# Centring and scaling of the layer norms in halves of 512 columns, in a three-layer block on one Trainium2 core

## The chip, the cores and the metric

The kernel runs on one core of one Trainium2 chip. The metric is device time in microseconds (us), lower is better. PE is the matrix engine, PEld its weight load, DVE the vector engine, ACT the scalar engine, POOL and SP the engines that mostly start transfers. Each engine runs its own list of instructions in order and waits for the others on semaphores.

## The reference

Three layers follow each other on 256 tokens of width 1024, all in float32: a gated linear attention with a convolutional MLP, an attention layer (forgetting and stick-breaking heads) with a SwiGLU, and a sliding-window layer with eight experts. What the change touches is the layer norm of the last two layers:

```python
def layer_norm(x, g, b):
    xf = x.astype(F32)
    mu = jnp.mean(xf, axis=-1, keepdims=True)
    xc = xf - mu
    var = jnp.mean(xc * xc, axis=-1, keepdims=True)
    return (xc * lax.rsqrt(var + LN_EPS) * g.astype(F32) + b.astype(F32)).astype(x.dtype)

for i in range(DEPTH_2):                    # 2
    h = fox_sb_mixer(...) or swa_mixer(...)
    x = layer_norm(DEEPNORM_ALPHA * x + h, ln_mix_g[i], ln_mix_b[i])
    h = swiglu(...) or moe_swiglu(...)
    x = layer_norm(DEEPNORM_ALPHA * x + h, ln_ffn_g[i], ln_ffn_b[i])
    x = x + jax.nn.sigmoid(x @ ple_w_gate[i]) * (p[i] @ ple_w_proj[i])
```

## The kernel before

The 256 tokens lie in two tiles of 128 (x[:, t, :]), the 1024 columns along the free dimension. Every product runs with operands split into a high and a low part (w_hi, w_lo of the weights, xt_hi, xt_lo of the activations), three matmuls for one. Weights stream in chunks of 128x2048 through rings of four: SP loads a chunk, ACT rounds it (w_hi, line 641), DVE makes the rest (w_lo, split_chunk, line 1200), PE uses it. A product needs the activations transposed: PE transposes 128x128 pieces into PSUM (L2174, four pieces of one half of 512 columns make one group, t_ready), ACT rounds the group (xt_hi), DVE subtracts (xt_lo, turned, L1212).

There are four layer norms, two tiles each. Three come from follow_norm: after ab_out, after ffn_down and after c_out. For each tile, add_half adds the second half of the product to x (L1288) and takes its statistics (L1290), then normalize(t, i, src) aggregates them (L1296), adds epsilon (L1298), lets ACT take the square root, meanwhile centres the tile and multiplies by the gain (L1301), takes the reciprocal (L1240), multiplies by it and adds the bias (L1303), drains, and raises t_source by 2. The fourth norm follows the experts: add_last and normalize(0), add_last(1), then in ple the two xt_lo groups of tile 0 and normalize(1).

DVE's order around them is written out by hand. After ab_out: norm of tile 0, of tile 1, then the four xt_lo groups (operand(5)) and the rest of p's operand. After ffn_down: tile 0; add_half of tile 1; between the two, first_operand (a chunk's split, xt_lo groups 0 and 1); the rest of tile 1's norm; then in ple the next split, xt_lo groups 2 and 3. After c_out: tile 0, tile 1, the four xt_lo groups (operand(9)), then the router's steps. After the experts, as said; then one split, groups 2 and 3, three splits.

PE's turn_tile(m, src, t) waits for t_source once for each half g, for 4m + 2t + g + 1, and transposes that half. So its two waits per tile are already there; before the change both are met by the one increment of 2. keep_warm issues dummy matmuls (L2179) between the tiles' transposes: 13 after ab_out, 11 after c_out, and 2 behind them. After ab_out PE then begins with the high parts (cols_chunk_high_first, L2134 and L2136) and needs xt_lo only for the last part (L2132). After ffn_down, ple(0) runs matmuls of tile 0 (L2056 to L2058), transposes tile 1, and goes on with the next chunk of tile 0. After c_out the router's matmuls are L2809, L2810 (high) and L2813 (low). After the experts, rows_high_first (L2540, L2541, then L2547 for w_lo) stands in ple(1). The lines of the change are 1300 to 1304.

Of the kernel before, what the change touches and what calls it, by code (L numbers as in the profile page):

```python
# [14 lines left out]
ALU = mybir.AluOpType  # L15
# [12 lines left out]
NB = 512  # L28
# [88 lines left out]
def build(nc, a, out, upto="end"):  # L117
# [27 lines left out]
    with ExitStack() as ctx:  # L145
# [13 lines left out]
        def sb(name, shape, dt=F32):  # L159

            t = at(name, shape, dt, free[0])
            free[0] += nbytes(shape)
            return t
# [11 lines left out]
        def S(name):  # L175

            if name not in sems:
                sems[name] = ctx.enter_context(nc.semaphore(name))
            return sems[name]
# [5 lines left out]
        x = sb("x", [P, NT, D])  # L185
# [15 lines left out]
        stat = sb("stat", [P, 16])  # L201
# [989 lines left out]
        def _(dve):  # L1191
            me = Place()
            dve.sem_inc(S("lo_ready"), RING)
            TT, STT, TS = dve.tensor_tensor, dve.scalar_tensor_tensor, dve.tensor_scalar
# [32 lines left out]
            def row(i):  # L1227
                dve.wait_ge(S(f"gain_landed{i % 2}"), 16 * (i // 2 + i % 2))
                return gain[:, i % 2, :]
# [3 lines left out]
            def inverse_root(tiles=slice(0, NT), meanwhile=None):  # L1233

                dve.drain().then_inc(S("ms_ready"), 1)
                if meanwhile:
                    meanwhile()
                dve.wait_ge(S("root_ready"), next(roots))
                a_, o = (slice(k + tiles.start, k + tiles.stop) for k in (2, 4))
                dve.reciprocal(stat[:, o], stat[:, a_])  # L1240
                dve.drain()
# [50 lines left out]
            def normalize(t, i, src):  # L1292

                g, b_ = row(i), row(i + 1)
                dve.drain()
                dve.bn_aggr(stat[:, 8 + 2 * t:10 + 2 * t], bn[:, t, :, :])  # L1296
                dve.drain()
                TS(stat[:, t:t + 1], stat[:, 9 + 2 * t:10 + 2 * t], LN_EPS, None, ALU.add)  # L1298

                def centred():  # L1300
                    STT(x[:, t, :], src[:, t, :], stat[:, 8 + 2 * t:9 + 2 * t], g, ALU.subtract, ALU.mult)  # L1301
                inverse_root(slice(t, t + 1), centred)
                STT(x[:, t, :], x[:, t, :], stat[:, 4 + t:5 + t], b_, ALU.mult, ALU.add)  # L1303
                dve.drain().then_inc(S("t_source"), 2)

            def follow_norm(name, i, between=None):

                (b0, c0, _, _, p0_), (b1, c1, _, _, p1_) = phase[name]
                round_to(c0 + len(p0_) + 2)
                wait_used(dve, c0 + len(p0_))  # L1310
                for t in range(NT):
                    add_half(0, t, acc[b0 % 2][t])
                dve.drain().then_inc(S(f"acc_free{b0 % 2}"), 1)
                round_to(c1 + len(p1_) + 2)
                for t in range(NT):
                    wait_tile(dve, name, t)
                    add_half(1, t, acc[b1 % 2][t])
                    if t == NT - 1:
                        dve.drain().then_inc(S(f"acc_free{b1 % 2}"), 1)
                        if between:  # L1320
                            between()
                    normalize(t, i, x)
                dve.sem_inc(S("gain_used"), 2)
# [11 lines left out]
            g = gain[:, 0, :]  # L1335
# [69 lines left out]
            for step in range(3):  # L1405
                for g in range(4):
                    src, dst = (step, step + 1) if g < 2 else (3 - step, 2 - step)
# [166 lines left out]
            if "ab_in" in live:  # L1574
# [46 lines left out]
                for h in range(8):  # L1621
                    dve.wait_ge(S("fox_t"), h + 1)
                    dve.tensor_copy(pt[:, h % 2, :], acc[va_b[0] % 2][h % 2][:, 0:SCW]).then_inc(S("fox_pt"), 1)
                    if h in (4, 6):
                        t = h // 2 - 2
# [43 lines left out]
            def ple(i, m, r=0):  # L1669

                blocks = phase[f"ple{i}"]
                if i:
                    turned(m, 0)
                    turned(m, 1)
                    normalize(1, m, y)
                    dve.sem_inc(S("gain_used"), 2)
                    round_to(blocks[0][1] + 3, r)
                    turned(m, 2)
                    turned(m, 3)
                    round_to(blocks[0][1] + 4, r)  # L1680
                else:
                    round_to(blocks[0][1] + 4, r)
                    turned(m, 2)
                    turned(m, 3)
                for q, (bb, cc, n0, n, ps) in enumerate(blocks[2:4]):
                    round_to(cc + len(ps) + 2, r)
                    for t in range(NT):
                        dve.wait_ge(S("sig_ready"), 4 * i + 2 * q + t + 1)
                        TT(sig[:, q, t, :], sig[:, q, t, :], p_out[:, t, n0:n0 + n], ALU.mult)
                        dve.drain()  # L1690
                        k = TT(x[:, t, n0:n0 + n], x[:, t, n0:n0 + n], sig[:, q, t, :], ALU.add)
                        if q and i == 0:
                            dve.drain().then_inc(S("t_source"), 2)
                        elif q and t == 0:
                            dve.drain().then_inc(S("ple_added"), 1)
                    dve.drain().then_inc(S("ple_added"), 1)
# [238 lines left out]
            if "moe" in live:  # L1935
# [92 lines left out]
                dve.drain()  # L2028
                add_last(0)
                normalize(0, 10, y)  # L2030
                add_last(1)
            if "ple1" in live:
# [853 lines left out]
```

## Time and profile before

| | us |
|---|---|
| median of 3 runs | 1815.37 (1813.89 to 1816.74) |
| the profiled execution | 1816.34 |
| its span, first to last instruction | 1814.6 |
| mean granted TensorE clock | 0.995 |
| PE / DVE / ACT busy | 98% / 75% / 61% |

A busy share is an average over the whole span; what matters for this change is who waits for whom in the few microseconds around each norm. The rows further below come from the page (shares and chain), from the chain of waits, from groups of instructions, from timelines (start, duration, engine, line, operation, and in brackets the idle time before it and what ended it) and from busy times by stretch.

### The profile page before, as it was taken

The page shows a single profiled execution, that of the slowest core. Times are in us where ns is not written, and L with a number is a line of the kernel's source. Part 1 is how long each engine was busy: PE and PEld are TensorE (multiplying, and loading weights), DVE is VectorE, ACT ScalarE, POOL GpSimd, SP SyncE. Part 2 cuts the span into 40 slices and gives each one's busy share as a digit, 9 for nine tenths or more (in the row PEclk, how much of TensorE's full clock was granted, in tenths as well). Part 3 has the DMA queues.
Part 4 walks back from the last instruction along what each step waited for, and adds up shares of the span by engine and source line. Part 5 has one row for each costly group of instructions (what it writes and reads, how often), then busy time and mean ns, then how long its engine had stood idle before and what let it go on. Part 6 is the DMA issues. An engine that isn't in the chain of part 4 may idle for free.

```text
span 1814.6 us, 23858 instructions
## 1 busy us (share of the span) xinstructions
PE 1781.8 (98%) x9708; PEld 1500.8 (83%) x9708; DVE 1369.8 (75%) x1199; ACT 1099.2 (61%) x976; POOL 71.5 (4%) x95
## 2 busy tenths in 40 slices
PE   8999999999999999999999999999999999999997
PEld 6979998897899877778788888888888888888886
DVE  4766784466644555689988888888898888888986
ACT  5545563474344344466776776777767777767764
POOL 2200000200000001000000000000000000000100
PEclk8999999999999999999999999999999999999999
DMA  7444556532455564269999999999999999999991
GB/s 260 163 170 151 185 174 221 168 119 98 170 185 184 186 208 140 72 229 386 331 397 380 340 399 357 368 390 349 383 380 345 400 354 368 391 353 377 403 348 71
DMA packets 250471, 496.76 MB, mean 274 GB/s; under 512 B 10630, under 2 KB 15818, under 8 KB 250368
## 3 DMA queue, kind: packets, MB, share of 16 engines
q1 hardware_dynamic: 244992, 477.30, 72.8%
q0 software_dynamic: 4944, 16.50, 2.5%
q8 instruction: 67, 1.10, 0.2%
q10 hardware_dynamic: 432, 1.57, 0.2%
q14 instruction: 36, 0.29, 0.0%
HBM read 489.56 MB, written 5.78 MB: 273 GB/s over the span
## 4 chain that ended last, share of the span: by engine, by line
PE 91%; DVE 5%; issue 1%; DVEq 1%; ACT 1%; DMA 0%; ACTq 0%; SPq 0%
PE psum L2737 17%; PE psum L2739 16%; PE psum L2738 16%; PE psum L2056 5%; PE psum L2151 5%; PE psum L2154 5%; PE psum L2153 5%; PE psum L2058 5%; PE psum L2057 5%; PE psum L2174 3%; DVE w_lo L1769 1%; PE psum L2134 1%; PE psum L2132 1%; PE psum L2136 1%; DVE w_lo L1200 1%
## 5 line engine op out<-in xcount | busy, mean ns | idle before, releaser
L641 ACT ACTIVATE w_hi<-w_raw 128x2048 fp32r<-128x2048 f32 (+1 forms) x357 | 641.0, 1835 | 99.7 <-PE psum L2058 60.4
L1769 DVE TENSOR_TENSOR w_lo<-w_raw,w_hi 128x2048 fp32r<-128x2048 f32 (+1 forms) x236 | 507.0, 2188 | 72.2 <-ACT w_hi L641 72.0
L1200 DVE TENSOR_TENSOR w_lo<-w_raw,w_hi 128x2048 fp32r<-128x2048 f32 (+2 forms) x121 | 266.0, 2230 | 122.3 <-ACT w_hi L641 120.0
L2737 PE MATMUL psum<-w_hi,xg_hi 128*128 128x512 f32 x892 | 356.4, 400 | 1.1 <-DVE w_lo L1769 1.1
L2739 PE MATMUL psum<-w_hi,xg_lo 128*128 128x512 f32 x892 | 352.4, 395 | 0.0
L2738 PE MATMUL psum<-w_lo,xg_hi 128*128 128x512 f32 x892 | 352.2, 395 | 0.0
L1769 DVE TENSOR_TENSOR w_lo<-raw_more,w_hi 128x2048 fp32r<-128x2048 f32 (+1 forms) x116 | 250.2, 2196 | 35.9 <-ACT w_hi L641 35.3
L641 ACT ACTIVATE w_hi<-raw_more 128x2048 fp32r<-128x2048 f32 (+1 forms) x118 | 210.5, 1823 | 16.9 <-PE psum L2739 12.6
L2151 PE MATMUL psum<-xt_hi,w_hi 128*128 128x256 f32 (+2 forms) x768 | 217.2, 283 | 0.0
L2154 PE MATMUL psum<-xt_hi,w_lo 128*128 128x256 f32 (+2 forms) x768 | 216.4, 282 | 0.0
L2153 PE MATMUL psum<-xt_lo,w_hi 128*128 128x256 f32 (+2 forms) x768 | 216.4, 282 | 0.0
L2739 PEld LDWEIGHTS psum<-w_hi,xg_lo 128*128 128x128 f32 x892 | 167.9, 188 | 39.6
L2737 PEld LDWEIGHTS psum<-w_hi,xg_hi 128*128 128x128 f32 x892 | 168.0, 188 | 39.3 <-DVE w_lo L1769 2.0
L2738 PEld LDWEIGHTS psum<-w_lo,xg_hi 128*128 128x128 f32 x892 | 168.1, 188 | 37.5
L2737 PE MATMUL psum<-w_hi,mh_hi 128*128 128x512 f32 x448 | 178.3, 398 | 0.6 <-DVE w_lo L1769 0.5
L2739 PE MATMUL psum<-w_hi,mh_lo 128*128 128x512 f32 x448 | 177.0, 395 | 0.0
L2738 PE MATMUL psum<-w_lo,mh_hi 128*128 128x512 f32 x448 | 176.8, 395 | 0.0
L2151 PEld LDWEIGHTS psum<-xt_hi,w_hi 128*128 128x128 f32 (+2 forms) x768 | 143.4, 187 | 1.3 <-issue 0.8
L2153 PEld LDWEIGHTS psum<-xt_lo,w_hi 128*128 128x128 f32 (+2 forms) x768 | 143.4, 187 | 0.5
L2154 PEld LDWEIGHTS psum<-xt_hi,w_lo 128*128 128x128 f32 (+2 forms) x768 | 143.3, 187 | 0.3
L641 ACT ACTIVATE mg<-psum 128x512 f32<-128x512 f32 x56 | 33.5, 598 | 167.8 <-PE psum L2739 167.8
L2737 PEld LDWEIGHTS psum<-w_hi,mh_hi 128*128 128x128 f32 x448 | 84.4, 188 | 20.2 <-issue 1.2
(438 smaller groups left out, 2285.0 us busy)
## 6 DMA issues: line engine op xcount, KB each, us to landing
w_raw<-in_moe_w_gate_up SPq DMA_DIRECT2D x150, 1024.0 KB, 8.7
raw_more<-in_moe_w_gate_up SPq DMA_DIRECT2D x74, 1024.0 KB, 8.6
w_raw<-in_moe_w_down SPq DMA_DIRECT2D x64, 1024.0 KB, 7.6
raw_more<-in_moe_w_down SPq DMA_DIRECT2D x32, 1024.0 KB, 7.4
w_raw<-in_w_up SPq DMA_DIRECT2D x22, 1024.0 KB, 5.6
w_raw<-in_ffn_w_gate_up SPq DMA_DIRECT2D x22, 1024.0 KB, 5.7
w_raw<-in_w_in SPq DMA_DIRECT2D x12, 1024.0 KB, 5.7
w_raw<-in_ab_w_in SPq DMA_DIRECT2D x12, 1024.0 KB, 5.3
```

The costliest lines, as they stand in the source:

```text
L641: return act.activation(o, i, func, **kw)
L1200: TT(w_lo[:, k % RING, 0:n], raw(slot, n), w_hi[:, k % RING, 0:n].bitcast(F32), ALU.subtract)\
L1769: TT(w_lo[:, at, 0:n], raw(slot, n), w_hi[:, at, 0:n].bitcast(F32), ALU.subtract).then_inc(S("lo_ready"), 1)
L2056: mm(o, hi(k, t), wh, start=(k == ps[0][0]), stop=False)
L2057: mm(o, hi(k, t), wl, start=False, stop=False)
L2058: m = mm(o, lo(k, t), wh, start=False, stop=(k == kmax))
L2151: mm(o, w_hi[:, slot, cols], xt_hi[:, k, :], start=(k == 0 and c_ % 2 == 0), stop=False, skip_group_check=True)
L2153: mm(o, w_hi[:, slot, cols], xt_lo[:, k, :], start=False, stop=False, skip_group_check=True)
L2154: m = mm(o, w_lo[:, slot, cols], xt_hi[:, k, :], start=False, stop=(k == KD - 1), skip_group_check=True)
L2737: mm(o, hi[:, q, :], wh, start=(q == first), stop=False)
L2738: mm(o, hi[:, q, :], wl, start=False, stop=False)
L2739: m = mm(o, lo[:, q, :], wh, start=False, stop=(q == last))
```

## The change

Centring and scaling of a tile are done in two halves of 512 columns (NB). The first half is centred while ACT takes the root, then scaled, drained and announced by raising t_source by 1; then the second half is centred, drained, scaled, drained and announced by 1 more. The transposes' waits are unchanged.

```diff
--- before.py
+++ after.py
@@ -1297,11 +1297,20 @@
                 dve.drain()
                 TS(stat[:, t:t + 1], stat[:, 9 + 2 * t:10 + 2 * t], LN_EPS, None, ALU.add)
 
-                def centred():
-                    STT(x[:, t, :], src[:, t, :], stat[:, 8 + 2 * t:9 + 2 * t], g, ALU.subtract, ALU.mult)
+                def centred(h=0):
+                    o = slice(h * NB, (h + 1) * NB)
+                    STT(x[:, t, o], src[:, t, o], stat[:, 8 + 2 * t:9 + 2 * t], g[:, o], ALU.subtract, ALU.mult)
+
+                def scaled(h):
+                    o = slice(h * NB, (h + 1) * NB)
+                    STT(x[:, t, o], x[:, t, o], stat[:, 4 + t:5 + t], b_[:, o], ALU.mult, ALU.add)
                 inverse_root(slice(t, t + 1), centred)
-                STT(x[:, t, :], x[:, t, :], stat[:, 4 + t:5 + t], b_, ALU.mult, ALU.add)
-                dve.drain().then_inc(S("t_source"), 2)
+                scaled(0)
+                dve.drain().then_inc(S("t_source"), 1)
+                centred(1)
+                dve.drain()
+                scaled(1)
+                dve.drain().then_inc(S("t_source"), 1)
 
             def follow_norm(name, i, between=None):
```

## Rows read from the trace of the kernel before

**Rows 1.** The profile's page: busy time of PE; the chain's shares by engine.
```profile
PE 1781.8 (98%) x9708; PEld 1500.8 (83%) x9708; DVE 1369.8 (75%) x1199; ACT 1099.2 (61%) x976; POOL 71.5 (4%) x95
...
PE 91%; DVE 5%; issue 1%; DVEq 1%; ACT 1%; DMA 0%; ACTq 0%; SPq 0%
```

**Rows 2.** Chain of waits, four stretches: start us, us, engine, tile, line.
```profile
465.69 1.09 PE psum L2174 x8
...
664.12 2.30 DVE w_lo L1200
...
781.04 1.09 PE psum L2174 x8
...
1788.50 2.30 DVE w_lo L1200
1790.85 1.20 PE psum L2547 x4
```

**Rows 3.** Groups of DVE by line and shape: count, busy us, mean ns, idle before.
```profile
L1303 DVE SCALAR_TENSOR_TENSOR x<-x,stat,gain 128x1024 f32<-128x1024 f32 x8 | 10.3, 1285 | 0.6
...
L1288 DVE SCALAR_TENSOR_TENSOR x<-x,psum 128x512 f32<-128x512 f32 x12 | 8.2, 683 | 12.7 <-PE psum L2058 12.4
...
L1691 DVE TENSOR_TENSOR x<-x,sig 128x512 f32<-128x512 f32 x8 | 5.5, 693 | 0.6
...
L1851 DVE SCALAR_TENSOR_TENSOR ys_lo<-psum,gslot,ys_hi 128x512 fp32r<-128x512 f32 x2 | 1.5, 745 | 0.0
```

**Rows 4.** Timeline of DVE, norm after ab_out, tile 0: start us, us.
```profile
457.20 0.21 DVE L1296 BATCH_NORM_AGGREGATE stat<-bn 128x2 f32<-128x12 f32 x1
457.49 0.15 DVE L1298 TENSOR_SCALAR stat<-stat 128x1 f32<-128x1 f32 x1
457.77 1.28 DVE L1301 SCALAR_TENSOR_TENSOR x<-x,stat,gain 128x1024 f32<-128x1024 f32 x1
458.97 0.15 DVE L1240 RECIPROCAL stat<-stat 128x1 f32<-128x1 f32 x1
459.21 1.28 DVE L1303 SCALAR_TENSOR_TENSOR x<-x,stat,gain 128x1024 f32<-128x1024 f32 x1
```

**Rows 5.** Timeline of ACT in the same norm: the square root.
```profile
457.70 0.20 ACT L641 ACTIVATE stat<-stat 128x1 f32<-128x1 f32 x1 [6.09 <-DVEq L1235]
```

**Rows 6.** Timelines of PE and DVE after ab_out: transposes, dummies, low parts.
```profile
460.58 1.09 PE L2174 MATMUL psum<-ident,x 128*128 128x128 f32 x8 [1.13 <-DVEq L1304]
...
466.62 0.60 PE L2179 MATMUL psum<-ones_tri 128*128 128x512 bf16 x2
...
471.29 0.99 PE L2132 MATMUL psum<-xt_lo,w_hi 128*128 128x256 f32 x7
...
465.82 2.48 DVE L1212 TENSOR_TENSOR xt_lo<-psum,xt_hi 128x512 fp32r<-128x512 f32 x4 [0.21 <-issue]
```

**Rows 7.** Timelines of DVE and PE after ffn_down.
```profile
659.24 1.28 DVE L1212 TENSOR_TENSOR xt_lo<-psum,xt_hi 128x512 fp32r<-128x512 f32 x2
...
660.63 0.44 PE L2056 MATMUL psum<-w_hi,xt_hi 128*128 128x512 f32 x1
...
666.46 0.50 PE L2056 MATMUL psum<-w_hi,xt_hi 128*128 128x512 f32 x1 [1.39 <-DVE w_lo L1200]
```

**Rows 8.** Timelines of DVE and PE after c_out.
```profile
775.97 0.69 DVE L1288 SCALAR_TENSOR_TENSOR x<-x,psum 128x512 f32<-128x512 f32 x1 [0.76 <-PE psum L2058]
...
781.44 2.48 DVE L1212 TENSOR_TENSOR xt_lo<-psum,xt_hi 128x512 fp32r<-128x512 f32 x4
...
784.34 1.08 PE L2813 MATMUL psum<-xt_lo,rw_hi 128*8 128x256 f32 x8
```

**Rows 9.** Timeline of PE after the experts: the first gate matmul.
```profile
1784.98 0.49 PE L2540 MATMUL psum<-w_hi,xt_hi 128*128 128x512 f32 x1 [2.32 <-DVE xt_lo L1212]
```

**Rows 10.** Busy us (instructions) of each engine by stretch; then granted clock, DMA share, GB/s.
```profile
665.00:670.00 5.00, 3.61 (x11) 2.78 (x11) 5.00 (x5) 4.98 (x5) 0.39 (x1) 0.71 0.79 234
670.00:675.00 5.00, 5.00 (x22) 4.07 (x21) 2.09 (x1) 0.65 (x1) 0.00 (x0) 0.95 1.01 371
```

## Prediction

> **What bounds the kernel now.** Read the page's first section for who is busy, then the chain of waits around each of the eight tile norms, then the timeline for the one wait that ends last there. The matrix engine (PE) is busy 98% of the span and is 91% of the chain; the vector engine (DVE) is only 5% of it [rows 1]. So nearly everywhere DVE time is covered and costs nothing. The norms are the exception. The chain runs through L1301 and L1303 at four places, and there DVE alone sets when PE goes on [rows 2]:
>
> A, after ab_out: tile 1's last norm step releases the eight transposes at 465.69. B, after ffn_down: DVE's queue behind the norm releases PE (the w_lo split of 664.12 ends and PE starts at 666.46 [rows 7]). C, after c_out: L1303 releases the transposes at 781.04. D, after the experts: the split of 1788.50 releases PE at 1790.85. The question is therefore what the change does to DVE's length in a norm, and whether the earlier first half pays for it.
>
> **Cost of one tile norm.** The change replaces two STT of 128x1024 by four of 128x512 and adds two drains, of which one carries a semaphore increment. No DMA, ACT or PE instruction is added or moved.
>
> The length of a half has no row of its own and must be inferred. The whole one takes 1285 ns. A 128x512 STT takes 683 ns with an immediate scalar (L1288) and a tensor-tensor of 512 columns from SBUF takes 693 (L1691), but the STT whose scalar is a column of SBUF, as in the norm, takes 745 (L1851) [rows 3]. That last is the nearest row: 1285 less 745 is 540 ns for 512 more columns. I take 0.745 us, and 0.69 as the lower end. Four halves less two wholes are then 4 x 0.745 - 2 x 1.285 = 0.41 us (lower end 0.19).
>
> A plain drain costs 0.08 us between two instructions (457.20 + 0.21 to 457.49), a drain that signals costs 0.13 (457.49 + 0.15 to 457.77); without a drain the next one starts 0.08 before the end (457.77 + 1.28 to 458.97) [rows 4]. The added drains give 0.08 + 0.13 = 0.21. **Per tile DVE is d = 0.62 us longer** (lower end 0.40; upper end 0.70, if a half takes 0.765, which is one row's excess over another, 20 ns, on top).
>
> What the first half gains: in the old order PE may start 2.81 us after L1301 begins (457.77 to 460.58, 0.09 of it release after 459.21 + 1.28) [rows 4, 6]. In the new: half centred and reciprocal by 0.67 + 0.24 = 0.91, half scaled 0.745, release 0.09: 1.75 us. The first four transposes may thus start 1.06 us earlier, and the last four start d = 0.62 later. Eight transposes take 0.93 us to issue (465.69 to 466.62 [rows 2, 6]), so four take 0.47.
>
> One cover shrinks: the square root on ACT hides under L1301. It starts 0.07 before L1301 and takes 0.20 [rows 5]; a half still covers it for 0.67 us. Cost nothing; without that cover 0.13 plus a semaphore.
>
> The Trainium skill, page "VectorE: DVE Perf Modes", section "The TRN2 errata — SBUF-src ops pay a fixed extra latency per instruction", gives (N+151)/0.96 ns for an fp32 tensor-tensor and warns that many small tiles pay the fixed part per tile. The tensor-tensor row agrees (693 ns), the norm's own STT does not (1285 ns against 1224). By the page's figure alone, an estimate, d would be 4 x 0.691 - 2 x 1.224 + 0.21 = 0.53 and the sum below 3.0.
>
> **The sum, place by place.** PE's own waits decide how much of d arrives.
>
> A. Tile 1's norm begins d later because tile 0's grew. PE waits for the second half: its last four transposes start 2d later than the eight do now, and four fewer are behind them: 2d - 0.47 = **+0.77**. The low parts that DVE makes next end at 465.82 + 2.48 + 2d, while PE wants them at 471.29 [rows 6]: over 2.9 us of cover less 1.24, free.
>
> B. DVE's xt_lo of tile 0 ends at 660.52 and PE goes on at 660.63 without having idled [rows 7]: the release is just in time, no slack, so d arrives at once. Then DVE normalizes tile 1 and only behind it splits the chunk for which PE waits at 666.46: 2d in all. The transposes don't matter: even 2d later than now they would end long before the split that PE waits for (its row shows 1.39 us of idle PE behind them) [rows 7]. **+1.24**. Queued behind the norm is exactly this split; SyncE's next loads wait for it too, but move only with PE.
>
> C. Tile 0's end doesn't matter: DVE idles 0.76 us there for PE before it takes tile 1 [rows 8], more than d. Tile 1: the last transposes end d - 0.47 = +0.15 later. But the DVE group xt_lo, 781.44 + 2.48, now ends at 783.92, and PE needs it at 784.34; less 0.12 of release there are 0.30 of slack. So d - 0.30 = **+0.32**, the larger of the two. The routing behind it is a chain of small steps, all passed on.
>
> D. Tile 0's transposes feed xt_lo groups that stand in DVE's queue behind tile 1's statistics, so they don't decide. Those statistics and the xt_lo that PE waits for at 1784.98 stand behind tile 0's norm [rows 9]: d. Then the split of 1788.50 stands behind tile 1's norm: 2d in all, **+1.24**, down to the last instruction.
>
> Sum: 7d - 0.77 = 7 x 0.62 - 0.77 = **+3.6 us**. With d at its lower end of 0.40 it is +2.0, at its upper of 0.70 +4.1. The profiled execution took 1816.34 us (span 1814.6) and would become 1819.9; the median of the runs, 0.97 lower, 1815.37, becomes **1819.0**.
>
> The granted clock is the second term. It fell from 2.4 to 1.2 GHz once near here: 0.71 in 665 to 670 and 0.95 in 670 to 675 [rows 10], after PE had idled 1.39 us before 666.46. That lost 0.29 x 5 + 0.05 x 5 = 1.7 us of matmul time. I leave it as it is in the sum: at B the fall comes anyway. D idles 2.32 us before 1784.98 at full clock, and would idle about 2.9.
>
> **Rivals.** What a run of this kernel can tell from no change is about 0.2%, 3.6 us, so my own forecast lies on that line.
>
> 1. The halves are cheap (0.69 us each, as L1288 and L1691): +2.0, **1817.3**. For it: most 512-column rows are at 0.68 to 0.69. Against: only those without a column as scalar.
> 2. The end is slower still: the clock falls once more. The longer waits of PE at D (2.9 us before the first gate matmul instead of 2.32, and 1.6 instead of 1.01 before 1790.85) are of the kind before which it fell at B. Price 1.7, **1820.7**. It decides if the granted clock between 1780 and 1795 is below 1.00. Against it: 2.32 us left it alone.
> 3. DVE's added time doesn't reach the end: waits that I read as DVE's end on something else (ACT's w_hi or xt_hi at B and D). Then A and C alone remain, 0 to 1.1 us, **1815.9**. Against: the releasers named in rows 2 and 9 are DVE's.
> 4. The change does as its words say and no more: the early half ends the wait. A and C gain 1.06 each, and at B four transposes fill the gap so that the clock holds (1.7): -3.8, **1811.5**. Against: every consumer but the transposes needs both halves, and PE runs them in order.
>
> **How the numbers follow.** Forecast 0.43, rival 1 0.16, rival 2 0.25, rival 3 0.12, rival 4 0.04. The forecast's own range, 1817.6 to 1820.2, straddles the line of 0.2%: I give 0.21 of it to "within" and 0.22 to "slower". Within 0.2%: 0.21 + 0.16 + 0.12 = 0.49; slower: 0.22 + 0.25 = 0.47; faster 0.04. The range reaches from the middle between rivals 3 and 1 (1816.6) to rival 2 with some scatter of runs, 1821.4.
>
> **What the profile after would show.** The half STTs at 745 ns, thirty-two of them; DVE's next instruction 3.47 us after L1301 begins, not 2.85 (1.28 + 0.13 after 459.21); at A the transposes in two groups of four, the second at about 466.9; at B PE's restart at 667.7; at C L2813 at about 0.3 later relative to what precedes it; at D restarts later by 0.6 and 1.2. Wrong would be: halves at 690 ns (rival 1), the last transposes on time, B and D restarting where they did, or a new stretch under full clock.

## The result and the profile after

The changed kernel took **1818.48 us** (median of 22 runs, 1817.56 to 1822.58) against 1815.38 for the kernel before (22 runs taken alongside, 1813.46 to 1818.94): 3.1 us more by the medians. The ratio is 1.002, with a 95% interval of 1.0014 to 1.0026, so between 2.5 and 4.7 us slower, 3.6 by the ratio itself. The forecast was 1819.0, +3.6. The profiled execution's span is 1819.1 us, against 1814.6.

The page of the changed kernel, busy time and chain, as in [rows 1]:

```profile
PE 1785.7 (98%) x9708; PEld 1502.7 (83%) x9708; DVE 1373.0 (75%) x1215; ACT 1099.9 (60%) x976; POOL 71.6 (4%) x95
...
PE 91%; DVE 6%; issue 1%; DVEq 1%; ACT 1%; DMA 0%; ACTq 0%; SPq 0%
```

DVE has 16 instructions more (1215, not 1199: two for each of eight tiles) and 3.2 us more of busy time; PE and ACT have the same instructions. DVE's share of the chain rose from 5% to 6%, which fits an addition that lies on the path; the timelines below show it.

The halves, by line and shape (count | busy us, mean ns | idle before), to be read beside [rows 3]. SCALAR_TENSOR_TENSOR, STT for short, combines an operand with a scalar and the result with a second operand:

```profile
L1306 DVE SCALAR_TENSOR_TENSOR x<-x,stat,gain 128x512 f32<-128x512 f32 x16 | 12.0, 752 | 1.2
L1302 DVE SCALAR_TENSOR_TENSOR x<-x,stat,gain 128x512 f32<-128x512 f32 x12 | 9.0, 752 | 1.5
L1302 DVE SCALAR_TENSOR_TENSOR x<-y,stat,gain 128x512 f32<-128x512 f32 x4 | 3.0, 752 | 0.5
```

Thirty-two halves at 752 ns. Timeline of DVE, norm after ab_out, tile 0, the counterpart of [rows 4]:

```profile
457.10 0.15 DVE L1298 TENSOR_SCALAR stat<-stat 128x1 f32<-128x1 f32 x1
457.38 0.75 DVE L1302 SCALAR_TENSOR_TENSOR x<-x,stat,gain 128x512 f32<-128x512 f32 x1
458.05 0.16 DVE L1240 RECIPROCAL stat<-stat 128x1 f32<-128x1 f32 x1
458.29 0.75 DVE L1306 SCALAR_TENSOR_TENSOR x<-x,stat,gain 128x512 f32<-128x512 f32 x1
459.16 0.75 DVE L1302 SCALAR_TENSOR_TENSOR x<-x,stat,gain 128x512 f32<-128x512 f32 x1
459.99 0.75 DVE L1306 SCALAR_TENSOR_TENSOR x<-x,stat,gain 128x512 f32<-128x512 f32 x1
460.87 0.69 DVE L1288 SCALAR_TENSOR_TENSOR x<-x,psum 128x512 f32<-128x512 f32 x1
```

The kernel before, its next instruction after the row of 459.21 in [rows 4]:

```profile
460.62 0.69 DVE L1288 SCALAR_TENSOR_TENSOR x<-x,psum 128x512 f32<-128x512 f32 x1
```

From the centring to the next tile's first instruction 3.49 us pass (457.38 to 460.87), where 2.85 passed before (457.77 to 460.62): **d = 0.64**. PE around that norm, tile 1, the counterpart of the rows of 465.69 and 466.62 in [rows 2, 6]:

```profile
464.86 0.66 PE L2183 MATMUL psum<-ident,x 128*128 128x128 f32 x4 [0.57 <-DVEq L1309]
466.56 0.66 PE L2183 MATMUL psum<-ident,x 128*128 128x128 f32 x4 [1.04 <-DVEq L1313]
467.05 0.59 PE L2188 MATMUL psum<-ones_tri 128*128 128x512 bf16 x2
```

The transposes now come in two groups of four. The first group is early: it starts 1.73 us after tile 1's centring began (463.13), where the eight started 2.80 after it before (462.89 to 465.69), so 1.07 earlier, as the 1.06 of the forecast. Then PE idles 1.04 us for the second half. What stands behind them waits for that one.

The restarts of PE after ffn_down and after the experts, the counterparts of [rows 7, 9] and of the row of 1790.85:

```profile
662.69 0.50 PE L2065 MATMUL psum<-w_hi,xt_hi 128*128 128x512 f32 x1
...
669.21 0.50 PE L2065 MATMUL psum<-w_hi,xt_hi 128*128 128x512 f32 x1 [1.82 <-DVE w_lo L1200]
...
1788.89 0.49 PE L2549 MATMUL psum<-w_hi,xt_hi 128*128 128x512 f32 x1 [1.65 <-DVE xt_lo L1212]
...
1795.40 1.20 PE L2556 MATMUL psum<-w_lo,xt_hi 128*128 128x512 f32 x4 [1.65 <-DVE w_lo L1200]
```

The row of 1790.85 in the kernel before, with its wait:

```profile
1790.85 1.20 PE L2547 MATMUL psum<-w_lo,xt_hi 128*128 128x512 f32 x4 [1.01 <-DVE w_lo L1200]
```

The releasers are the same DVE instructions as before, only later: 1.82 us of idle PE ahead of 669.21 where there were 1.39, and 1.65 ahead of 1795.40 where there were 1.01. Ahead of 1788.89 the idle time is shorter than before, 1.65 instead of 2.32, since PE came late out of the projection, at a lower clock (see the clock, below).

To compare kernels place by place, every time is taken from the first L1296 of that norm (tile 0's aggregate) to an event on PE: A to the first matmul of the up-projection, B to the restart behind the w_lo split, C to the first gather of the experts (L2694 before, L2703 after), D to the second group of gate matmuls (L2540 before, L2549 after). These are differences of start times in the timelines. Two profiles of the kernel before and three of the change stand in the table:

```
us                          A      B      C      D     sum of differences
before (two profiles)     10.21  14.77  18.33  13.85
                          10.20  14.76  18.31  13.84
changed (three profiles)  11.03  15.68  18.90  15.21
                          11.02  15.67  18.88  15.12
                          11.03  15.68  18.90  15.12
difference                +0.82  +0.91  +0.57  +1.3   +3.6
```

The rest of the 4.5 us between the two profiled spans, 0.9 us, lies outside these places: the stretch from A to B is 1.4 us longer (experiment 8) and that from B to C 0.2, the stretch ahead of A is 0.4 shorter and the experts' 0.3.

### The profile page after: what moved, and what is told of

It is laid out like the page before. It is cut to its first block, busy times and chain, and to the rows that moved or that the text cites. A ratio compares the mean times of both kernels' runs of the same rounds, so it can differ in the third digit from the quotient of the medians.

```text
span 1819.1 us, 23890 instructions
## 1 busy us (share of the span) xinstructions
PE 1785.7 (98%) x9708; PEld 1502.7 (83%) x9708; DVE 1373.0 (75%) x1215; ACT 1099.9 (60%) x976; POOL 71.6 (4%) x95
## 4 chain that ended last, share of the span: by engine, by line
PE 91%; DVE 6%; issue 1%; DVEq 1%; ACT 1%; DMA 0%; ACTq 0%; SPq 0%
PE psum L2746 16%; PE psum L2748 16%; PE psum L2747 16%; PE psum L2160 5%; PE psum L2065 5%; PE psum L2163 5%; PE psum L2162 5%; PE psum L2067 5%; PE psum L2066 5%; PE psum L2183 3%; DVE w_lo L1778 1%; PE psum L2145 1%; PE psum L2141 1%; PE psum L2143 1%; DVE w_lo L1200 1%
## 5 line engine op out<-in xcount | busy, mean ns | idle before, releaser
L2748 PEld LDWEIGHTS psum<-w_hi,mh_lo 128*128 128x128 f32 x448 | 84.3, 188 | 19.9
```

The lines of the kernel that those rows point to most:

```text
L2748: m = mm(o, lo[:, q, :], wh, start=False, stop=(q == last))
```

## The experiments

**1. The kernel before, a second profile.** No edit.

> The kernel before, once more, for its trace alone. In the profiles so far the SwiGLU's up-projection took 22.78 us a turn before and 23.04 after (DVE's product of gate and value, start to start), 1.4 us over the stage, with the same instructions on PE. If that is a property of the change's code, this profile shows 22.78 again, and 23.04 is seen only with the change. If it differs from run to run, either value may come.

Measured: 1813.84 us in its one run, span 1812.1. A turn of the up-projection (from one of DVE's products of gate and value to the next) took 22.78. The places are those of the first profile to 0.02 us (table above), but the span is 2.5 shorter. The difference goes with the granted clock: 1.2 us of it lie ahead of A, where the clock differs in the first 20 us (below, busy time by engine, then clock, DMA share and GB/s; first this profile's row, then the first profile's) and 1.5 us between B and C, where the clock stays full after ffn_down here and fell in [rows 10]:

```profile
0.00:20.00 20.00, 13.73 (x47) 8.67 (x48) 11.26 (x13) 10.39 (x15) 8.39 (x25) 0.83 0.91 326
```

```profile
0.00:20.00 20.00, 12.65 (x42) 8.17 (x43) 10.23 (x11) 9.28 (x13) 8.01 (x24) 0.74 0.90 322
```

So one kernel's executions differ by some 3 us with its clock, and only the places in the timelines tell smaller things.

**2. The change, timed again.** No edit.

> The changed kernel once more. Theory (DVE's own length): a tile norm holds DVE 0.64 us longer and the sum over the four places is 0.8 + 1.3 + 0.3 + 1.3 = 3.7 us over the kernel before, 1819.1 by its median. Rival (the profile's whole difference of 4.5 us is the change's, the slower turns of the up-projection included): 4.5 us or more, 1820. The profile's turns of the up-projection tell whether that part belongs to it.

Measured: 1818.26 us median against 1815.47; ratio 1.0017 (1.0008 to 1.0026), so 1.5 to 4.7 us: the time alone excludes neither expectation, but the places repeat. The turn of the up-projection was 23.04 again, and this time an earlier stage, w_up, had the slower slots too (the time from one matmul to the next: 0.1201 us instead of 0.1186), with a span of 1820.8. Whether the slots belong to the change was not settled by it; experiment 8 returns to it.

**3. The halves, one notice.**

```diff
                 scaled(0)
-                dve.drain().then_inc(S("t_source"), 1)
+                dve.drain()
                 centred(1)
                 dve.drain()
                 scaled(1)
-                dve.drain().then_inc(S("t_source"), 1)
+                dve.drain().then_inc(S("t_source"), 2)
```

> The halves as in the change, but both announced together at the end of the second. Theory (DVE's own length, the early half saves only four transposes' 0.47 us where PE waits for them): d is 0.59 us here, since one drain signals no more. A: 2d = 1.2; B 1.2; C: now the eight transposes decide, 0.6; D 1.2: together 4.2 us over the kernel before, 0.5 more than the change. Rival (the early announcement itself costs, by breaking the transposes into two waits of PE): less than the change, about 3.2 us over the kernel before.

Measured: 1820.61 us, ratio 1.0026 (1.0016 to 1.0037), which is 4.7 us by the ratio; the interval would hold the rival's 3.2 too, so the places decide: A +1.16, B +0.81, C +0.86, D +2.7, of which 1.5 is a fall of the clock (below). Without the early notice PE takes all eight transposes at the end, in the profile of this kernel:

```profile
465.76 1.09 PE L2183 MATMUL psum<-ident,x 128*128 128x128 f32 x8 [1.79 <-DVEq L1313]
466.69 0.60 PE L2188 MATMUL psum<-ones_tri 128*128 128x512 bf16 x2
```

Against the change the notice is worth 0.34 at A (1.16 less 0.82): four transposes' 0.47 less 0.1, since its signal makes a drain 0.05 longer in each of two tiles. At C it is worth 0.29: without it the eight transposes decide there (0.59, and 0.26 of a stall that the change has too), with it the low parts do, as the prediction had it. At B it is worth nothing, and costs the 0.1. So the early notice pays what the theory said, a third of a microsecond at two places, and the halves cost several times that.

**4. The whole tile, DVE held as long by something else.**

```diff
+                dve.reduce_sum(stat[:, 15:16], src[:, t, 0:540], AX_X)
                 inverse_root(slice(t, t + 1), centred)
```

> The whole tile as in the kernel before, no halves, but with one DVE instruction more in each tile norm (a sum over 540 columns whose result nobody reads), which holds DVE some 0.64 us. It prices lateness alone. Theory: A 2 x 0.64 = 1.3, B 1.3, C 0.64, D 1.3: 4.5 us over the kernel before. Rival (the halves cost by something other than DVE's time, for instance what DVE and ACT or PE do to each other while halves are read and written): this kernel is nearly as fast as the kernel before, under 2 us over it.

Measured: 1819.87 us, ratio 1.0029 (1.0019 to 1.0040). Timeline of DVE, after ab_out, tile 0:

```profile
456.93 0.70 DVE L1302 TENSOR_REDUCE stat<-x 128x1 f32<-128x540 f32 x1
457.76 1.28 DVE L1301 SCALAR_TENSOR_TENSOR x<-x,stat,gain 128x1024 f32<-128x1024 f32 x1
458.96 0.16 DVE L1240 RECIPROCAL stat<-stat 128x1 f32<-128x1 f32 x1
459.20 1.28 DVE L1304 SCALAR_TENSOR_TENSOR x<-x,stat,gain 128x1024 f32<-128x1024 f32 x1
460.61 0.69 DVE L1288 SCALAR_TENSOR_TENSOR x<-x,psum 128x512 f32<-128x512 f32 x1
```

The added row holds DVE 0.62 us per tile, about d (L1288 of tile 1 comes 4.04 us after the aggregate of 456.57, and 3.42 after in the kernel before). Places: A +1.24, B +1.18, C +0.61, D +1.24, 4.3 us in all, where 4.5 were expected. No halves, no early notice, and the cost is there: lateness of DVE alone makes it. (The ratio says 5.3 us, 3.4 to 7.3.)

**5. Tile 1 alone in halves.**

```diff
+                def whole():
+                    STT(x[:, t, :], src[:, t, :], stat[:, 8 + 2 * t:9 + 2 * t], g, ALU.subtract, ALU.mult)
-                inverse_root(slice(t, t + 1), centred)
-                scaled(0)
+                inverse_root(slice(t, t + 1), centred if t else whole)
+                if t:
+                    scaled(0)
...
+                else:
+                    STT(x[:, t, :], x[:, t, :], stat[:, 4 + t:5 + t], b_, ALU.mult, ALU.add)
+                    dve.drain().then_inc(S("t_source"), 2)
```

> Tile 1 alone in halves, tile 0 whole. Theory (each tile norm adds 0.64 us of DVE, four transposes saved at A): A 0.64 - 0.47 = 0.2, B 0.6, C 0.3, D 0.6: 1.8 us over the kernel before. Rival (only the queue behind tile 1 counts, so nearly all of the change's cost is here): over 3 us. Second question, the slots of PE: both profiles of the change showed the up-projection's 256-column matmuls at 0.1200 us each (a turn of 23.04), the kernel before, the one with one notice and the late whole tile at 0.1187 (22.78). If the split release of tile 1's transposes after ab_out brings it about, this kernel shows 23.04 and costs 1.4 us more, 3.2.

Measured: 1818.52 us (kernel before alongside: 1815.76), ratio 1.0021 (1.0012 to 1.0030). Places: A +0.19, B +0.28, C +0.27, D +1.25: 2.0 us, for 1.8 expected. A and C are as forecast (0.2, 0.3). B is 0.3 lower: the kernel before has a stall of 0.48 us in DVE's queue there, at L1301 (shown in experiment 6), and this kernel has none. D is 0.6 higher, and 0.4 of it is the opposite, a longer stall. This profile's split after the experts:

```profile
1790.41 2.29 DVE L1200 TENSOR_TENSOR w_lo<-w_raw,w_hi 128x2048 fp32r<-128x2048 f32 x1 [0.68 <-issue]
```

In the kernel before that instruction waits 0.28 for "issue", here 0.68. The other 0.2 lie between the aggregates of the two tiles (6.97 us, 6.74 before): the transposes of tile 0 came late, the clock having fallen in the projection ahead (0.66 in 1775 to 1780). The timed ratio is above the profile's 2.0 us: 3.8, with an interval of 2.2 to 5.4; that gap stays open, and the time alone would not refute the rival's 3 us. The rival (nearly everything behind tile 1) is refuted at A and C, by the timelines. The turn was 22.78 in spite of the split release of tile 1.

**6. The change everywhere but after ab_out.** (whole as in experiment 5.)

```diff
-                inverse_root(slice(t, t + 1), centred)
+                inverse_root(slice(t, t + 1), whole if i == 4 else centred)
+                if i == 4:
+                    STT(x[:, t, :], x[:, t, :], stat[:, 4 + t:5 + t], b_, ALU.mult, ALU.add)
+                    dve.drain().then_inc(S("t_source"), 2)
+                    return
                 scaled(0)
```

> The change at the other three norms, the whole tile after ab_out. Theory: the change less A's 0.8: B 0.9 to 1.3, C 0.3 to 0.6, D 1.3, 2.9 us over the kernel before. If the slower slots of the up-projection come from the split release after ab_out, they are gone too (a turn of 22.78), and the trace shows 1.4 us less between A and B than that of the change. Rival (the slots belong to the longer code, not to that place): 23.04 stays.

Measured: 1819.89 us (before 1815.76), ratio 1.0017 (1.0008 to 1.0026), 3.1 us. The turn is 22.78. Places: A 0.00, B +1.26, C +0.55, D +1.27: 3.1 us, for 2.9. The cost is the sum of separate places. B is +1.26 here and +0.91 in the change, although its norm is the same there. The row that explains it (this kernel's DVE timeline after ffn_down):

```profile
652.05 0.75 DVE L1302 SCALAR_TENSOR_TENSOR x<-x,stat,gain 128x512 f32<-128x512 f32 x1 [0.47 <-issue]
```

The kernel before has this stall too, at its L1301, in both profiles:

```profile
652.61 1.29 DVE L1301 SCALAR_TENSOR_TENSOR x<-x,stat,gain 128x1024 f32<-128x1024 f32 x1 [0.48 <-issue]
```

The change does not; there the centring begins without it:

```profile
653.81 0.15 DVE L1298 TENSOR_SCALAR stat<-stat 128x1 f32<-128x1 f32 x1
654.10 0.75 DVE L1302 SCALAR_TENSOR_TENSOR x<-x,stat,gain 128x512 f32<-128x512 f32 x1
```

**7. The opposite edit: whole tiles without the drain.** The drain moves behind tile 1, where it frees the gain rows (the last two lines of the edit stand in two places, follow_norm and ple).

```diff
-                STT(x[:, t, :], x[:, t, :], stat[:, 4 + t:5 + t], b_, ALU.mult, ALU.add)
-                dve.drain().then_inc(S("t_source"), 2)
+                STT(x[:, t, :], x[:, t, :], stat[:, 4 + t:5 + t], b_, ALU.mult, ALU.add).then_inc(S("t_source"), 2)
...
-                dve.sem_inc(S("gain_used"), 2)
+                dve.drain().then_inc(S("gain_used"), 2)
```

> The kernel before with the opposite edit: whole tiles, and t_source raised by the scaling itself instead of by a drain behind it (the drain moves behind the norm of tile 1, where it frees the gain rows). Theory: what counts is how long a tile norm holds DVE; tile 0's is 0.21 us shorter (0.13 of drain, 0.08 of overlap), PE's release after tile 1 0.04: A -0.25, B -0.2, C 0, D -0.2: -0.7 us, 1814.8, faster than the kernel before by less than can be told. Rival (drains are free, the next instruction waits anyway): no difference in the trace, start to start.

Measured: 1814.54 us against 1815.76, ratio 0.9993 (0.9984 to 1.0002). Its DVE timeline after ab_out:

```profile
457.43 1.28 DVE L1301 SCALAR_TENSOR_TENSOR x<-x,stat,gain 128x1024 f32<-128x1024 f32 x1
458.63 0.16 DVE L1240 RECIPROCAL stat<-stat 128x1 f32<-128x1 f32 x1
458.87 1.28 DVE L1303 SCALAR_TENSOR_TENSOR x<-x,stat,gain 128x1024 f32<-128x1024 f32 x1
460.07 0.68 DVE L1288 SCALAR_TENSOR_TENSOR x<-x,psum 128x512 f32<-128x512 f32 x1
```

The next instruction starts 2.64 us after the centring, not 2.85: the 0.21 that were forecast. A -0.25 as expected; B -0.65, of which 0.35 is the stall that is absent here, so -0.3 where -0.2 was expected; C -0.01. D is +0.31, not -0.2: the clock had fallen while PE worked on the projection ahead of it (granted 0.81 in 1770 to 1775 and 0.85 in 1775 to 1780), so the transposes came late and DVE idled 0.49 us for ACT's xt_hi. Timed once more:

> Whole tiles without the drain ahead of the announcement, timed again, since it is the fastest so far and the first five rounds (ratio 0.9993, 0.9984 to 1.0002) don't part it from the kernel before. Theory: 0.5 to 1.2 us faster than the kernel before, 3 to 4 us faster than the change. Rival (drains are free): as the kernel before.

Measured: 1814.03 us against 1816.36, ratio 0.9993 (0.9984 to 1.0002) again. A and B are the same to 0.01, D +0.64 with the same early fall of the clock. Twice the median is below the kernel before, by 1.2 and 2.3 us, and twice the interval touches 1. Against the change it is clearly faster; against the kernel before that isn't shown.

**8. What the slower slots are.** A third dummy matmul behind the last transposes after ab_out, and further profiles of two kernels.

```diff
-                keep_warm(2, 3)
+                keep_warm(3 if m == 5 else 2, 3)
```

> The change, with three dummy matmuls instead of two between the last transposes after ab_out and the up-projection; nothing on DVE differs. It moves the moment at which PE's long unbroken run of 256-column matmuls begins. Theory (the slots of 0.1200 us instead of 0.1187 are a rhythm into which PE falls at the start of that run, by its timing, and keeps): the turn is 22.78 or 23.04, and if 22.78, the stretch from A to B is 1.4 us shorter than the change's and the kernel 1.2 us faster than it (the dummy costs 0.2). Rival (the slower slots belong to the split release itself): 23.04 stays and the kernel is 0.2 us slower than the change.

Measured: 1818.31 us (before 1816.36), ratio 1.0015 (1.0006 to 1.0024); turn 22.78 and A to B 1.4 us shorter than in the first profile of the change, as the theory said; A 0.22 longer than the change's, the price of the dummy. But the kernel isn't the 1.2 us faster that the theory wanted: the change itself had 1818.26 and 1818.48.

> The changed kernel a third time, one look. If the slower slots of the up-projection are fixed by the code's timing, the turn is 23.04 again; if they vary by execution, it may be 22.78. The extra stall of 0.26 us in DVE's queue in the routing (at FIND_INDEX8), seen in both profiles of the change and in none of the kernel before, is expected again at the same instruction, and none at L1302 after ffn_down.

Measured: the changed kernel unedited, 1820.62 us in its one run, and the turn is **22.78**. DVE's product of gate and value in two profiles of the same kernel, first the one shown above:

```profile
514.34 1.22 DVE L1657 TENSOR_TENSOR uv<-ug,psum 128x1024 f32<-128x1024 f32 x1 [4.30 <-PE psum L2163]
537.38 1.22 DVE L1657 TENSOR_TENSOR uv<-ug,psum 128x1024 f32<-128x1024 f32 x1 [4.30 <-PE psum L2163]
```

and the third profile:

```profile
513.99 1.22 DVE L1657 TENSOR_TENSOR uv<-ug,psum 128x1024 f32<-128x1024 f32 x1 [4.18 <-PE psum L2163]
536.77 1.22 DVE L1657 TENSOR_TENSOR uv<-ug,psum 128x1024 f32<-128x1024 f32 x1 [4.17 <-PE psum L2163]
```

23.04 and 22.78 a turn, at a full clock both times. So the slower slots, 1.4 us between A and B of the first profile, vary from execution to execution of one kernel, and the change does not bring them by necessity; the third dummy's 22.78 proves nothing about timing either. They were seen in two of three profiles of the change and one of two of experiment 9's kernel, and in none of the two of the kernel before and the seven of the other variants. So whether the change makes them likelier, and carries some of their 1.4 us in its median, is not shown. DVE's stall in the routing was at the same instruction in all three (0.26 us at FIND_INDEX8, in this third profile):

```profile
790.04 0.09 DVE L1968 MATCH_VALUE_LOAD route_u<-route 128x8 f32 x1
790.38 0.17 DVE L1968 FIND_INDEX8 route_u<-route 128x8 uint32<-128x8 f32 x1 [0.26 <-issue]
```

It goes with the change's code, and makes C +0.57 where L2822 itself (L2813 before) is only 0.27 later. The variants agree: experiment 5's kernel has no such stall, and its C is +0.27; experiment 6's has one of 0.34 at another instruction of the routing (L1983), and its C is +0.55.

**9. Scaling alone in halves.** Centring stays whole, and the drain moves as in experiment 7.

```diff
-                STT(x[:, t, :], x[:, t, :], stat[:, 4 + t:5 + t], b_, ALU.mult, ALU.add)
-                dve.drain().then_inc(S("t_source"), 2)
+                for h in range(2):
+                    o = slice(h * NB, (h + 1) * NB)
+                    STT(x[:, t, o], x[:, t, o], stat[:, 4 + t:5 + t], b_[:, o], ALU.mult, ALU.add).then_inc(S("t_source"), 1)
```

> Centring whole; scaling in halves without drains, each raising t_source by 1 itself. Theory: tile 0's norm holds DVE 0.07 us less, the last transposes of tile 1 are released about 0.1 later but are four fewer: A -0.44, B +0.1, C -0.2, D +0.1: -0.5 us, 1814.9. Rival (an early half pays by itself): -1 us or more at each of A and C, 1813.4. Slots: if two releases of tile 1's transposes after ab_out bring about the 0.1200 us, they are seen here (23.04 a turn, +1.4).

Measured: 1815.08 us (before 1815.76), ratio 1.0000 (0.9991 to 1.0009). A -0.42, B -0.05, C -0.32, D -0.02: 0.8 us less by the places, for 0.5 forecast, and too little for the time to show. DVE's next instruction starts 2.78 us after the centring (457.26 to 460.04), so each tile norm is 0.07 shorter than in the kernel before, by the drain that is gone, and 0.14 longer than experiment 7's whole tile without a drain. Against that kernel, the fair comparison, the early release wins 0.17 at A and 0.31 at C; B and D are blurred by the stall at L1301, which is here again (0.47), and by experiment 7's clock. Once more:

> Scaling alone in halves, a second look. Its first profile had 23.04 a turn in the up-projection. Fixed by the code's timing: 23.04 again. Varying by execution: 22.78 is possible.

Measured: 22.78 a turn this time, after 23.04 in the first profile (1815.08 us, span 1813.3): varying by execution. The places A, B, C repeat to 0.02; D was +0.77 with the clock fallen ahead of it, which eats the 0.8.

## Why the prediction was right, point by point

**What bounds.** That DVE is alone on the path at the four norms, and there in its own length, held: experiment 4 buys a like loss with an instruction that has nothing to do with the change. With d = 0.64 the terms come to 0.81 at A, 1.28 less the vanished stall's 0.35 at B, and 1.28 at D; measured are 0.82, 0.91 and 1.27.

**The length of a half**, taken from the 745 ns row and not from the many at 683 to 693, measured 752. d was 0.62 by the sum and is 0.64. Rival 1, cheap halves, falls with it. The reason given, a column of SBUF as scalar, fits the rows at both widths (1285, 752, 745 with it; 683 at 512 without). The kernel before also has a row at 1024 without it, with an immediate as scalar:

```profile
L1359 DVE SCALAR_TENSOR_TENSOR logd<-psum,tmp 128x1024 f32<-128x1024 f32 x1 | 1.2, 1224 | 7.0 <-ACT tmp L641 7.0
```

So the column goes with 61 or 62 ns at either width; it was not tried by itself. By the formula for an fp32 tensor-tensor of the Trainium skill, page "VectorE: DVE Perf Modes", section "The TRN2 errata — SBUF-src ops pay a fixed extra latency per instruction", a half would have been 691 ns; it measured 752, so the row was the better guide.

**The drains** cost what the rows said: 0.12 us from the first half's end to 459.16 and 0.08 to 459.99, and taking one away gave 0.21 back (experiment 7).

**A**: +0.77 forecast, +0.82 measured. The gain of the early half is four transposes at most, as experiment 3 shows by taking it away (0.34).

**B**: +1.24 forecast, +0.91 measured. DVE's own stretch from L1302 to the end of the split is longer by 1.25, as the sum had it. What the sum did not see is the 0.35 us by which the stall at L1301, present in both profiles of the kernel before, went away. It was in the trace as an "issue" wait, and was silently taken as fixed. One of the times named as signs was added up wrongly: 667.7 for B's restart adds 1.24 to the old time and leaves out A's own 0.77, so by the sum itself it is 668.5; the profile has 669.21, by the slower slots (1.4) less the 0.4 ahead of A and the 0.3 of B.

**C**: +0.32 forecast for L2813, +0.27 measured; then 0.28 of new stall, +0.57 in all.

**D**: +1.24 forecast, +1.27 to +1.36 measured.

The two code-bound stalls, -0.35 and +0.28, nearly cancelled: the sum was 3.6, the places give 3.6, the medians 3.1. That the total fits so closely is in part this luck, and in part that clock and slots, which the sum left as they were, move single runs by as much as the whole effect.

**The clock** (rival 2) came in part, and not at its price. Its sign, a granted clock below 1.00 between 1780 and 1795, was met in two of three profiles of the change; the first of them:

```profile
1775.00:1780.00 5.00, 2.89 (x13) 2.00 (x12) 3.99 (x7) 4.94 (x4) 0.00 (x0) 0.95 0.59 212
1780.00:1785.00 5.00, 5.00 (x17) 4.01 (x16) 4.38 (x9) 1.92 (x4) 0.00 (x0) 0.71 0.01 3
```

After ffn_down it fell in one of two profiles of the kernel before and in all three of the change; PE's stretch from the restart to DVE's next product (L1689 before, L1698 after) then grew from 9.3 to 10.9 us, and to 12.1 in the third. At D it fell in two of three, but in the projection, where PE had room: D is +1.36 and +1.27 there, and +1.27 in the third, where it stayed full although PE idled the longer time that the rival feared:

```profile
1788.58 0.50 PE L2549 MATMUL psum<-w_hi,xt_hi 128*128 128x512 f32 x1 [2.75 <-DVE xt_lo L1212]
```

In experiment 8's kernel with the third dummy, behind the same 2.75 us, it fell further on among the gate matmuls (0.66 in 1790 to 1795), and D was +1.56. When it fell at the first of them, as in experiment 3's profile, behind 2.32 us of idle PE, it cost 1.5:

```profile
1785.59 0.79 PE L2549 MATMUL psum<-w_hi,xt_hi 128*128 128x512 f32 x1 [2.32 <-DVE xt_lo L1212]
1786.18 0.63 PE L2550 MATMUL psum<-w_hi,xt_lo 128*128 128x512 f32 x1
1786.60 0.63 PE L2549 MATMUL psum<-w_hi,xt_hi 128*128 128x512 f32 x1
```

The same idle of 2.32 us left the clock alone in both profiles of the kernel before [rows 9]. And experiment 6, with B as long as the change's, kept the full clock there. Whether the change makes falls likelier is not settled. Among the timed runs the kernel before reached a mean clock of 0.997 in 9 of 21, 12 of 33 and 5 of 21, and the change in none of 22 and none of 11, which chance alone would hardly give. But the fastest kernel, experiment 7's, didn't reach it in 22 runs either, so being late is not what decides, and what does was not found.

**Rivals 3 and 4** fall: the releasers stayed DVE's, and every consumer but the transposes waited for the second half.

## What to carry to other kernels

An early notice is worth only the work that can be done on the first part and that would otherwise stand behind the last: here four transposes, 0.47 us, once. Splitting an instruction to give it lengthens the producer, and where the producer is on the path, everything queued behind it pays, at each place and for each tile: price the length of the producer first. The cheapest form tried was a notice on the instruction itself, no drain, and only the last step halved (experiment 9): it holds DVE 0.14 us longer per tile than the whole tile without a drain, wins a little at two places, and its time could not be told from the kernel before. Dropping the drain did as much without any halves (experiment 7).

## What the runs showed of the hardware

- A 128x512 STT with a column of SBUF as scalar takes 752 ns (745 with one operand in PSUM), 128x1024 takes 1285; with an immediate and one operand in PSUM, 683 and 1224.
- A plain drain between two DVE instructions costs 0.15 to 0.16 us from start to start against none, and 0.05 more when it raises a semaphore: the next instruction starts 0.08 us before the end of the last one without a drain, 0.08 behind it with one, 0.12 to 0.13 behind it with the semaphore.
- Stalls of DVE named "issue", 0.26 to 0.68 us, sit at instructions that depend on the code ahead of them, repeat in every profile of the kernels that were profiled twice or more, and vanish, change or come at another instruction when the code around them changes (0.48 at L1301, 0.36 at L1298 with experiment 4's added row, none in the change).
- PE's 256-column matmuls ran at 0.1187 or 0.1200 us each at full clock, for a whole stage, in executions of the same kernel (the change, and experiment 9's). It moves the up-projection, some 1,050 matmuls, by 1.4 us, and the first two profiles of the change alone would have put that down to it. What decides between the two was not found.
